# Two-block transformer kernel: weight slots spaced 16 bytes further, operands of two stages shifted, strided weights in one down projection, reversed tokens in another

## The chip, the cores and the metric

The kernel runs on 1 core of one Trainium2 chip. The metric is the device time of one execution in microseconds (us), as a median over runs. TensorE (PE in the rows) does the matmuls; PEld is its weight load. DVE is VectorE, ACT is ScalarE, POOL is GpSimd, SP is SyncE, which issues the weight DMAs.

## What is computed

Two blocks over x of 512 tokens by 1024 features, all float32. Each holds two layers. What matters here is that every matrix product has a large weight matrix, and that the changed stages are the merged output projection and the down projections:

```python
for i in range(2):                                   # first block
    ...
    x = x + rms_norm(merged @ w_out[i], norm_mix_post[i])
    ff = (silu(h @ w_ffn_gate[i]) * (h @ w_ffn_up[i])) @ w_ffn_down[i]    # 2816 -> 1024
    x = x + rms_norm(ff, norm_ffn_post[i])
    e = (p[i] @ w_ple_proj[i]) * sigmoid(x @ w_ple_gate[i])
...
for layer in range(2):                               # second block
    h = h + (hybrid_attention_mixer if layer == 0 else recurrent_mixer)(...)
    u = causal_depthwise_conv(rms_norm(h) @ w_up, conv_w, conv_b)
    g, val = split(u)
    h = h + (gelu(g) * val) @ w_down                  # 3072 -> 1024
```

## The kernel before

Activations lie in SBUF feature-major: a tile `[128, 512]` holds 128 features of all 512 tokens. The weights come as a list of 502 units (`unit_list`), each `[128, 1024]` float32 (4096 bytes per partition): up to 8 blocks of 128 contraction rows by 128 output features. The host lays them out in one array (the helper near L2545).

A unit goes through four slots (`SLOTS = 4`). SP issues the DMA of a unit into `WRAW[:, slot, :]` when the unit four places earlier has been used (L607, semaphore `unit_used`). ACT rounds it to `WHI` in the type fp32r (L1228, `split_of`), POOL computes the remainder `WLO = WRAW - WHI` into the same bytes as `WRAW` (L2383), both three units ahead of their use. Operands are kept as a rounded half and a remainder too: `HH/HL` for the normed input, `MGH/MGL` for the merged branches, `F1H/F1L` and `F2H/F2L` for the hidden layers of the two kinds of feed-forward, `OBH/OBL` (258 columns, so rows 1032 bytes apart) for the Fourier branch, and so on. A product is three matmuls for each block, the helper `three`:

```python
pe.matmul(out_, WHI[w_at], x_hi, start=first, stop=False)      # L621
pe.matmul(out_, WHI[w_at], x_lo, start=False, stop=False)      # L622
return pe.matmul(out_, WLO[w_at], x_hi, start=False, stop=last)  # L623
```

The first argument after the output is stationary (it is loaded by LDWEIGHTS, 128 columns), the second is streamed (512 tokens). In the rows, names behind `<-` stand as streamed operand, stationary operand. `tile(st, j, k, ...)` runs the blocks of one unit into a PSUM bank and marks the unit used. It is called by `out_y`, which runs the stage kinds `out_y` and `residual`: eight output tiles, for F2 three units each (24 blocks). Other stages call `part` or `tile_part`.

The F2 stage stands twice in the program: after the first convolutional feed-forward (from 2443.3 to 2573.8 us of the span, 8 x 24 x 3 = 576 matmuls), whose `residual` has a gain for the next norm, and after the second (3005.3 to 3135.8 us, again 576), whose `residual` has none. F1 stands twice (528 matmuls each), MG twice (192 each).

Work tiles are placed by hand: `place` for the fixed ones (X, HH, HL, WRAW/WLO, WHI, ...), `work(name, shape, at)` at a number of KB behind a base. All start at multiples of 128 bytes before, and a slot is 4096 bytes. `GT` holds a gate in two branch stages: VectorE writes it, ACT applies tanh (L1326, L1373), VectorE reads it (L1877, L1937).

Other places that the prediction speaks of: L697 and L703 (Fourier transform over tokens; L703's stationary operand is `PG[:, s, :, P]`, four columns 1024 bytes apart), L879 (attention scores in plain float32), L913 (probabilities times values, 64 stationary columns), L1055 to L1057 and L1072 to L1074 (the attention input projection, 256 streamed columns), L1115 (sums: 128 stationary columns, one streamed), L1892 and L1894 (the unfolding of the Fourier branch; L1892 writes `MG[:, n, 0:257]` forward, L1894 writes `MG[:, n, 511:256:-1]` backward), L2214 (a tap of the convolution, which reads `U`, rows 2064 bytes apart, at offsets of 4 bytes).

Of the kernel before, what the change touches and what calls it, by code (L numbers as in the profile page):

```python
# [67 lines left out]
BANKS = 4  # L68
LAG = 3
LINE = 128  # L70

F32 = mybir.dt.float32
F32R = mybir.dt.float32r
# [98 lines left out]
class Stage:  # L172
# [3 lines left out]
    def __init__(self, kind, reps, units, tiles, per, *, u0, t0, base, rb=None, width=0, where=None, src=None, dst=None,  # L176
                 gain=None, n=0, stat=False, y=None, gy=None, t=0, made=None, kt=0, first=False, last=False, op=0, mode=None,
                 heads=0, comps=1, out=None, l=0, proj=None, rope=None, qk=None, att=None, norm=None, taps=0, ahead=None, put_off=False):
        self.kind, self.reps, self.units, self.tiles, self.per = kind, reps, units, tiles, per
        self.u0, self.t0, self.base = u0, t0, base  # L180
        self.rb, self.width, self.where = rb, width, where
        self.src, self.dst, self.gain, self.n, self.stat = src, dst, gain, n, stat
        self.y, self.gy, self.t, self.made, self.kt = y, gy, t, made, kt
        self.first, self.last, self.op, self.mode, self.heads, self.comps = first, last, op, mode, heads, comps
        self.out, self.l, self.proj, self.rope, self.qk, self.att = out, l, proj, rope, qk, att
        self.norm, self.taps, self.ahead, self.put_off = norm, taps, ahead, put_off
        self.tables, self.halves, self.begun, self.cq = None, False, False, None

    def at(self, signal, k, r=0):

# [183 lines left out]
def build(nc, wall, wnyq, xin, pin, posi, posc, cols, consts, gmask, dft, dftc, dil, lamv, out_):  # L374


    with ExitStack() as ctx:
# [20 lines left out]
        YH = place("YH", [P, DT, SEQ], at=h_at + 16 * KB)  # L398
        HQ = place("HQ", [P, 16, SEQ], at=h_at)
        w_at = base[0]  # L400
        WRAW = place("WRAW", [P, SLOTS, BLOCKS * P])
        WLO = place("WLO", [P, SLOTS, BLOCKS * P], F32R, at=w_at)
        WHI = place("WHI", [P, SLOTS, BLOCKS * P], F32R)
        SG = place("SG", [P, 4, SEQ])
        SQ, TM = place("SQ", [P, 2, SEQ]), place("TM", [P, 2, SEQ])
        ACC = place("ACC", [P, SEQ])
# [26 lines left out]
        def work(name, shape, at, dt=F32):  # L433
            return place(name, shape, dt, at=s_at + int(at * KB))
# [11 lines left out]
        VCT, VR, KRAW = work("VCT", [P, SEQ], 98), work("VR", [P, ST, P], 26), work("KRAW", [P, SEQ], 8)  # L446
        RBQ, RBK = work("RBQ", [P, SEQ], 76), work("RBK", [P, SEQ], 78)
        PT, PTG, BT = work("PT", [P, 4, SEQ], 28), work("PTG", [P, 4, SEQ], 40), work("BT", [P, 2, ST, 3 * P], 28)
        OCR, OCR2, OAR, GT = work("OCR", [P, 2, SEQ], 22), work("OCR2", [P, 1, SEQ], 48), work("OAR", [P, 4, SEQ], 36), work("GT", [P, SEQ], 100)
        CQH, CQL = work("CQH", [P, 4, SEQ], 28, F32R), work("CQL", [P, 4, SEQ], 36, F32R)  # L450
        QA, KA, VA = work("QA", [P, MLA_H, SEQ], 10), work("KA", [P, MLA_H, SEQ], 44), work("VA", [P, ST, SEQ], 0)
        OCH, OCL = work("OCH", [P, 4, SEQ], 60, F32R), work("OCL", [P, 4, SEQ], 68, F32R)
        OAH, OAL = work("OAH", [P, 4, SEQ], 60, F32R), work("OAL", [P, 4, SEQ], 68, F32R)
        MGH, MGL = work("MGH", [P, DT, SEQ], 28, F32R), work("MGL", [P, DT, SEQ], 44, F32R)
        F1H, F1L = work("F1H", [P, FT1, SEQ], 0, F32R), work("F1L", [P, FT1, SEQ], 44, F32R)
        POH, POL, PROWS = work("POH", [P, 2, SEQ], 92, F32R), work("POL", [P, 2, SEQ], 96, F32R), work("PROWS", [P, ST, PLE], 88)
        YP = work("YP", [P, DT, SEQ], 16)
        QKV, PT2 = work("QKV", [P, ST, 3 * DM], 0), work("PT2", [P, TURNED, SEQ], 48)
        BT2, SGY = work("BT2", [P, 4, SEQ], 72), work("SGY", [P, 2, SEQ], 96)
# [155 lines left out]
        def _(pe):  # L615
# [9 lines left out]
            def tile(st, j, k, r, src, kt, k0=0, ready=None, start=True, stop=True):  # L625

                weights(st.unit(j, r))
                s = st.unit(j) % SLOTS
                if start:
                    pe.wait_ge(bank_free[st.bank(k)], st.use(k, r))  # L630
                hi, lo = src
                for i in range(kt):
                    if ready is not None:
                        pe.wait_ge(S["operand_ready"], ready + k0 + i + 1)
                    mm = three(ps[st.bank(k)][:, :], (slice(None), s, slice(i * P, i * P + P)), hi[:, k0 + i, :],
                               lo[:, k0 + i, :], start and i == 0, stop and i == kt - 1)
                mm.then_inc(unit_used, 1)

            def norm(st):
# [568 lines left out]
        def _(act):  # L1208
# [103 lines left out]
            def fourier_branch(st):  # L1312
                att = st.att
                for q in range(att.heads * ST + DEPTH + 1):
                    n, odd = divmod(q, 2)
                    if q < att.heads * ST:
                        exponentials(att, q)
                    if DEPTH <= q < att.heads * ST + DEPTH:
                        turned_copies(att, q - DEPTH)
                    if q < 2 * DT:  # L1320
                        split_of(st, q)
                    if q <= QT:
                        cq_square(st.cq, q)
                    if n < DT and not odd:
                        act.wait_ge(bank_free[st.bank(3 * n)], st.use(3 * n) + 1)
                        act.activation(GT[:, :], GT[:, :], ACT.Tanh, scale=0.5).then_inc(S["gate_ready"], 1)  # L1326
                    elif n < DT:
                        k = 3 * n + 2
                        act.wait_ge(unit_used, st.unit(2 * n + 1) + 1)
                        if n >= 2:  # L1330
                            act.wait_ge(bank_free[st.bank(k - 7)], st.use(k - 7) + 1)
                        act.activation(TM[:, n % 2, 0:UH], ps[st.bank(k)][:, 0:UH], ACT.Copy, scale=0.5).then_inc(bank_free[st.bank(k)], 1)
# [26 lines left out]
            def branch_mla(st):  # L1359
                att = st.att  # L1360
                for q in range(att.heads * ST + DEPTH + 1):
# [8 lines left out]
                        split_of(st, 2 * r)  # L1370
                    if part_ == 1:
                        act.wait_ge(bank_free[st.bank(2 * r)], st.use(2 * r) + 1)
                        act.activation(GT[:, :], GT[:, :], ACT.Tanh, scale=0.5).then_inc(S["gate_ready"], 1)  # L1373
                    if part_ == 2:
                        split_of(st, 2 * r + 1)
                heads_hi(att, unit_used, st.unit(st.units - 1) + 1)
# [361 lines left out]
        def _(dve):  # L1738
# [123 lines left out]
            def fourier_branch(st):  # L1862
# [3 lines left out]
                for q in range(att.heads * ST + DEPTH + 1):  # L1866
# [6 lines left out]
                    if 1 <= n <= DT and not odd:  # L1873
                        dve.wait_ge(S["gate_ready"], st.at("gate_ready", n))
                        dve.wait_ge(S["unfolded"], st.at("unfolded", n))
                        dve.wait_ge(bank_free[st.bank(3 * n - 2)], st.use(3 * n - 2) + 1)
                        dve.scalar_tensor_tensor(MG[:, n - 1, :], GT[:, :], 1.0, MG[:, n - 1, :], ALU.add, ALU.mult).then_inc(S["product_ready"], 1)  # L1877
                    if q == 2 * DT:
                        dve.wait_ge(S["cq_summed"], st.cq.at("cq_summed", 1))
                        for k, width in ((0, Q_LORA), (1, KV_LORA)):  # L1880
# [2 lines left out]
                    if n < DT and not odd:  # L1883
                        fold_of(st, 2 * n)
                        dve.wait_ge(unit_used, st.unit(2 * n) + 1)
                        if n:
                            dve.wait_ge(S["product_ready"], st.at("product_ready", n))
                        scaled(st, 3 * n, 0, GT[:, :])
                    elif n < DT:
                        even, odd_ = 3 * n + 1, 3 * n + 2  # L1890
                        dve.wait_ge(bank_free[st.bank(odd_)], st.use(odd_) + 1)
# [23 lines left out]
            def branch_mla(st):  # L1915
                att = st.att
                dve.wait_ge(S["factor_rows_ready"], st.at("factor_rows_ready", 0))
                for q in range(att.heads * ST + DEPTH + 1):
# [9 lines left out]
                        dve.scalar_tensor_tensor(MG[:, t, :], TM[:, 0, :], 0.5, MG[:, t, :], ALU.mult, ALU.add).then_inc(S["product_ready"], 1)  # L1928
                    if r < DT - 2 and part_ == 1:
                        dve.wait_ge(unit_used, st.unit(2 * r) + 1)  # L1930
                        scaled(st, 2 * r, 0, GT[:, :])
                    if r < DT - 2 and part_ == 2:
                        dve.wait_ge(unit_used, st.unit(2 * r + 1) + 1)
                        dve.wait_ge(S["gate_ready"], st.at("gate_ready", r + 1))
                        if r:
                            dve.wait_ge(S["product_ready"], st.at("product_ready", r))
                        dve.scalar_tensor_tensor(TM[:, 0, :], GT[:, :], 1.0, ps[st.bank(2 * r + 1)][:, :], ALU.add, ALU.mult)\  # L1937
                           .then_inc(bank_free[st.bank(2 * r + 1)], 1)
                heads_lo(att, st.u0 + st.units - 1, ST)

# [589 lines left out]
def packed_weights(inputs):  # L2530

    w = np.zeros((NU, P, BLOCKS * P), np.float32)
    for n, (name, layer, r0, rows, c0, cols) in enumerate(UNITS):
# [11 lines left out]
            w[n, :, :rows // P * cols] = a.reshape(rows // P, P, cols).transpose(1, 0, 2).reshape(P, -1)  # L2545
        else:
            a = a[r0:r0 + rows, c0:c0 + cols]
            w[n, :, :rows // P * cols] = a.reshape(rows // P, P, cols).transpose(1, 0, 2).reshape(P, -1)
    return w


# [66 lines left out]
```

## Time and profile before

| what | us |
|---|---|
| median of 2 runs | 3156.12 (3155.55 to 3156.69) |
| the profiled execution | 3148.41 |
| its span, first to last instruction | 3146.6 |
| PE busy in the span | 3020.4 (96%) |
| POOL busy | 1476.7 (47%) |
| mean granted clock of TensorE | 0.982 of full |

Busy time of PE counts each matmul to its modelled end, which overlaps the next one; the pace of matmuls is read from their starts, or from the chain of waits, where each piece counts from one start to the next.

### The profile page before, as it was taken

Reading aid. Unit: us, or ns where it says so; the run is one execution under the profiler, and the core shown is the slowest. Engines: PE = TensorE matmul, PEld = TensorE weight load, DVE = VectorE, ACT = ScalarE, POOL = GpSimd, SP = SyncE. Lnnn points to the kernel's source line nnn. Section 1 sums busy time; section 2 is a strip of 40 time slices with the busy share of each in tenths; the row PEclk is TensorE's granted clock in tenths of the full one; section 3 lists DMA queues with packets and bytes.
Section 4 is the critical chain, followed back from the end, with each engine's and each line's share of the span. In section 5 each row is a group of like instructions: output and inputs, shape, how many; then the busy total and the mean of one; then the engine's idle time right before and its main releaser. Section 6 shows DMA issues by size and latency. Waiting matters only on the chain.

```text
span 3146.6 us, 41609 instructions
## 1 busy us (share of the span) xinstructions
PE 3020.4 (96%) x15016; PEld 2465.3 (78%) x15016; DVE 1188.1 (38%) x1996; ACT 1296.4 (41%) x2023; POOL 1476.7 (47%) x851
## 2 busy tenths in 40 slices
PE   8999998999989999999999989889999999999999
PEld 6886786888868776777888779767888877788887
DVE  5444334221062444434221250443555127555510
ACT  3454443232242555443222342563555227344421
POOL 3565455444454654555444444443444434344443
PEclk9999999999989999999999999999999999999999
DMA  3222232333322231332333222102333332233232
GB/s 128 68 81 74 70 121 83 95 96 98 107 74 88 68 93 56 94 101 87 100 93 103 84 86 90 58 1 74 94 100 93 100 94 74 81 100 99 94 98 89
DMA packets 78523, 274.38 MB, mean 87 GB/s; under 512 B 8504, under 2 KB 12216, under 8 KB 78400
## 3 DMA queue, kind: packets, MB, share of 16 engines
q1 hardware_dynamic: 74064, 266.05, 27.5%
q10 hardware_dynamic: 4336, 6.63, 0.6%
q8 instruction: 86, 1.41, 0.2%
q14 instruction: 37, 0.30, 0.0%
HBM read 270.54 MB, written 2.10 MB: 87 GB/s over the span
## 4 chain that ended last, share of the span: by engine, by line
PE 88%; DVE 6%; ACT 3%; issue 1%; POOL 1%; DMA 1%; ACTq 0%; DVEq 0%; SPq 0%
PE ps L621 25%; PE ps L623 24%; PE ps L622 24%; PE ps L879 3%; PE ps L890 2%; PE ps L913 2%; DVE HL L1806 1%; PE ps L1055 1%; PE ps L1057 1%; PE ps L1056 1%; POOL WLO L2383 1%; PE ps L697 1%; DVE ps L1795 1%; DVE X L1798 1%; ACT WHI L1228 1%
## 5 line engine op out<-in xcount | busy, mean ns | idle before, releaser
L2383 POOL TENSOR_TENSOR WLO<-WRAW,WHI 128x1024 fp32r<-128x1024 f32 x471 | 1138.3, 2421 | 1315.7 <-ACT WHI L1228 1315.4
L621 PE MATMUL ps<-HH,WHI 128*128 128x512 f32 x2288 | 909.3, 397 | 46.3 <-DVE HL L1806 23.9
L623 PE MATMUL ps<-HH,WLO 128*128 128x512 f32 x2288 | 896.9, 392 | 0.0
L622 PE MATMUL ps<-HL,WHI 128*128 128x512 f32 x2288 | 896.5, 392 | 0.0
L1228 ACT ACTIVATE WHI<-WRAW 128x1024 fp32r<-128x1024 f32 x471 | 494.8, 1053 | 330.9 <-DMA WRAW<-wall 330.7
L621 PEld LDWEIGHTS ps<-HH,WHI 128*128 128x128 f32 x2288 | 433.0, 189 | 154.7 <-POOL WLO L2383 25.2
L623 PEld LDWEIGHTS ps<-HH,WLO 128*128 128x128 f32 x2288 | 432.9, 189 | 91.3
L622 PEld LDWEIGHTS ps<-HL,WHI 128*128 128x128 f32 x2288 | 433.5, 189 | 88.0 <-issue 1.0
L2214 DVE SCALAR_TENSOR_TENSOR ps<-U,COLS,ps 128x512 f32<-128x512 f32 x192 | 145.1, 755 | 143.8 <-ACT ps L1603 129.7
L1829 DVE TENSOR_TENSOR ACC<-ACC,SQ 128x512 f32<-128x512 f32 x80 | 78.2, 978 | 307.4 <-ACT SQ L1472 293.4
L621 PE MATMUL ps<-F2H,WHI 128*128 128x512 f32 x384 | 149.4, 389 | 0.0
L622 PE MATMUL ps<-F2L,WHI 128*128 128x512 f32 x384 | 149.4, 389 | 0.0
L623 PE MATMUL ps<-F2H,WLO 128*128 128x512 f32 x384 | 149.4, 389 | 0.0
L621 PE MATMUL ps<-F1H,WHI 128*128 128x512 f32 x352 | 137.1, 390 | 0.0
L623 PE MATMUL ps<-F1H,WLO 128*128 128x512 f32 x352 | 137.0, 389 | 0.0
L622 PE MATMUL ps<-F1L,WHI 128*128 128x512 f32 x352 | 136.9, 389 | 0.0
L2465 POOL TENSOR_SCALAR SG<-SG,RS 128x512 f32<-128x512 f32 (+3 forms) x132 | 84.5, 651 | 94.5 <-DVE RS L2066 78.6
L2106 DVE TENSOR_TENSOR X<-X,ps 128x512 f32 x32 | 22.0, 687 | 248.3 <-PE ps L623 248.2
L1055 PE MATMUL ps<-WHI,HH 128*128 128x256 f32 x352 | 101.9, 289 | 6.3 <-POOL WLO L2383 6.3
L1500 ACT ACTIVATE F1H<-TM 128x512 f32 (+1 forms) x44 | 27.8, 631 | 192.8 <-DVE TM L2125 192.8
L1946 DVE TENSOR_TENSOR TM<-ps,RBX 128x512 f32<-128x512 f32 x44 | 30.4, 691 | 189.8 <-PE ps L623 189.8
L1056 PE MATMUL ps<-WLO,HH 128*128 128x256 f32 x352 | 101.3, 288 | 0.0
(367 smaller groups left out, 4684.1 us busy)
## 6 DMA issues: line engine op xcount, KB each, us to landing
WRAW<-wall SPq DMA_DIRECT2D x502, 512.0 KB, 3.6
DFT<-dft ACTq DMA_DIRECT2D x4, 516.0 KB, 5.5
XROWS<-xin SPq DMA_DIRECT2D x2, 1024.0 KB, 7.2
y<-YROWS ACTq DMA_DIRECT2D x4, 512.0 KB, 2.6
PROWS<-pin ACTq DMA_DIRECT2D x2, 512.0 KB, 4.0
DIL<-dil ACTq DMA_DIRECT2D x1, 768.0 KB, 4.9
COLS<-cols ACTq DMA_DIRECT2D x1, 294.5 KB, 6.5
POSI<-posi SPq DMA_DIRECT2D x1, 256.0 KB, 11.7
```

The source lines that it names most:

```text
L621: pe.matmul(out_, WHI[w_at], x_hi, start=first, stop=False)
L622: pe.matmul(out_, WHI[w_at], x_lo, start=False, stop=False)
L623: return pe.matmul(out_, WLO[w_at], x_hi, start=False, stop=last)
L879: pe.matmul(score_bank(st, q, c)[:, 0:(b - a) * P], qs, ks, start=True, stop=True).then_inc(S["scores_ready"], 1)
L890: mm = pe.transpose(turn_ps[c][:, k * P:(k + 1) * P], probs_at(st, q, c)[:, k * P:(k + 1) * P], IDENT[:, :])
L1055: pe.matmul(o, HH[:, t, at], whi, start=t == 0, stop=False)
L1056: pe.matmul(o, HH[:, t, at], wlo, start=False, stop=False)
L1228: act.activation(WHI[:, s, :], WRAW[:, s, :], ACT.Copy).then_inc(wt_hi, 1)
L1829: dve.tensor_tensor(ACC[:, :], ACC[:, :], SQ[:, slot, :], ALU.add).then_inc(S["square_added"], 1)
L2214: dve.scalar_tensor_tensor(d, U[:, k, n - 1 - m:n - 1 - m + SEQ], w(n - 1 - m), src, ALU.mult, ALU.add)\
L2383: pool.tensor_tensor(WLO[:, s, :], whole, WHI[:, s, :].bitcast(F32), ALU.subtract).then_inc(wt_lo, 1)
L2465: pool.tensor_scalar(p, p, RS[:, s:s + 1], 1.0, ALU.mult, ALU.mult).then_inc(S["probs_ready"], 1)
```

## The change

Four edits of addresses and access patterns. No instruction is added, removed or moved: the sequence of instructions and waits on each engine is the same, apart from the name of one tile.

1. Each slot of WRAW, WLO and WHI is followed by 16 unused bytes, so slots are 4112 bytes apart and begin at 0, 16, 32 and 48 bytes behind a multiple of 128 (the sum over four slots is padded to the next multiple of 128).
2. MGH and MGL move 64 bytes down; F1H and F1L move 32 bytes up. F1L then ends where other tiles began, so POH, POL and PROWS move by 512 bytes, and GT is split into GTC and GTA at other places.
3. The weights of the first F2 stage (`ffn_w_down_2`, layer 0) are laid out by the host with the eight blocks interleaved, and the stationary operand takes every eighth element (128 elements, 32 bytes apart).
4. In the second F2 stage the streamed operand and the PSUM output run backward over the 512 tokens; weights are contiguous there.

```diff
+STAGGER = 16
...
+        self.interleaved, self.backwards = src == "F2" and gain is not None, src == "F2" and gain is None
...
-        WRAW = place("WRAW", [P, SLOTS, BLOCKS * P])
-        WLO = place("WLO", [P, SLOTS, BLOCKS * P], F32R, at=w_at)
-        WHI = place("WHI", [P, SLOTS, BLOCKS * P], F32R)
+        unit = slice(0, BLOCKS * P)
+        slots = [P, SLOTS, BLOCKS * P + STAGGER // 4]
+        WRAW = place("WRAW", slots)[:, :, unit]
+        WLO = place("WLO", slots, F32R, at=w_at)[:, :, unit]
+        base[0] += -base[0] % LINE
+        WHI = place("WHI", slots, F32R)[:, :, unit]
+        base[0] += -base[0] % LINE
...
-        OCR, OCR2, OAR, GT = work("OCR", [P, 2, SEQ], 22), work("OCR2", [P, 1, SEQ], 48), work("OAR", [P, 4, SEQ], 36), work("GT", [P, SEQ], 100)
+        OCR, OCR2, OAR = work("OCR", [P, 2, SEQ], 22), work("OCR2", [P, 1, SEQ], 48), work("OAR", [P, 4, SEQ], 36)
+        GTC, GTA = work("GTC", [P, SEQ], 50), work("GTA", [P, SEQ], 82)
...
-        MGH, MGL = work("MGH", [P, DT, SEQ], 28, F32R), work("MGL", [P, DT, SEQ], 44, F32R)
-        F1H, F1L = work("F1H", [P, FT1, SEQ], 0, F32R), work("F1L", [P, FT1, SEQ], 44, F32R)
-        POH, POL, PROWS = work("POH", [P, 2, SEQ], 92, F32R), work("POL", [P, 2, SEQ], 96, F32R), work("PROWS", [P, ST, PLE], 88)
+        MGH, MGL = work("MGH", [P, DT, SEQ], 28 - 1 / 16, F32R), work("MGL", [P, DT, SEQ], 44 - 1 / 16, F32R)
+        F1H, F1L = work("F1H", [P, FT1, SEQ], 1 / 32, F32R), work("F1L", [P, FT1, SEQ], 44 + 1 / 32, F32R)
+        POH, POL, PROWS = work("POH", [P, 2, SEQ], 92.5, F32R), work("POL", [P, 2, SEQ], 96.5, F32R), work("PROWS", [P, ST, PLE], 88.5)
...
-                    mm = three(ps[st.bank(k)][:, :], (slice(None), s, slice(i * P, i * P + P)), hi[:, k0 + i, :],
-                               lo[:, k0 + i, :], start and i == 0, stop and i == kt - 1)
+                    at = slice(i, None, BLOCKS) if st.interleaved else slice(i * P, i * P + P)
+                    tokens = slice(None, None, -1) if st.backwards else slice(None)
+                    mm = three(ps[st.bank(k)][:, tokens], (slice(None), s, at), hi[:, k0 + i, tokens],
+                               lo[:, k0 + i, tokens], start and i == 0, stop and i == kt - 1)
...
-            w[n, :, :rows // P * cols] = a.reshape(rows // P, P, cols).transpose(1, 0, 2).reshape(P, -1)
+            order = (1, 2, 0) if name == "ffn_w_down_2" and layer == 0 else (1, 0, 2)
+            w[n, :, :rows // P * cols] = a.reshape(rows // P, P, cols).transpose(*order).reshape(P, -1)
```

## Rows read from the trace of the kernel before

**Rows 1.** The page, section 1: busy us, share of the span, instructions.

```profile
span 3146.6 us, 41609 instructions
PE 3020.4 (96%) x15016; PEld 2465.3 (78%) x15016; DVE 1188.1 (38%) x1996; ACT 1296.4 (41%) x2023; POOL 1476.7 (47%) x851
```

**Rows 2.** The page, section 4: the chain that ended last.

```profile
PE 88%; DVE 6%; ACT 3%; issue 1%; POOL 1%; DMA 1%; ACTq 0%; DVEq 0%; SPq 0%
```

**Rows 3.** The chain of waits inside the first F2 stage.

```profile
by line: PE ps L622 33.4%; PE ps L621 33.4%; PE ps L623 33.3%
```

**Rows 4.** Stretches MG, F1, F2, F2: us, busy of PE, PEld, DVE, ACT, POOL, PEclk.

```profile
442.00:486.00 44.00, 44.00 (x195) 36.24 (x193) 8.39 (x11) 16.08 (x24) 21.53 (x9) 1.00 0.32 102
744.50:864.00 119.50, 119.50 (x530) 98.93 (x529) 8.10 (x12) 33.67 (x41) 57.42 (x24) 1.00 0.35 106
2443.30:2573.80 130.50, 130.50 (x577) 108.09 (x576) 18.37 (x27) 35.10 (x41) 59.53 (x25) 1.00 0.32 97
3005.30:3135.80 130.50, 130.50 (x577) 107.94 (x575) 8.40 (x12) 24.67 (x25) 54.98 (x23) 1.00 0.28 85
```

**Rows 5.** The chain in order of time, by start: 256 streamed columns in fp32r.

```profile
1872.42 0.12 PE ps L1072
...
1874.82 0.12 PE ps L1074
```

**Rows 6.** Groups by line and form: busy us, mean ns; counts of three-matmul products.

```profile
L621 PE MATMUL ps<-HH,WHI 128*128 128x512 f32 x2288 | 909.3, 397 | 46.3 <-DVE HL L1806 23.9 <-POOL WLO L2383 15.0 <-DVE HL L1809 6.8
L621 PE MATMUL ps<-F2H,WHI 128*128 128x512 f32 x384 | 149.4, 389 | 0.0
L621 PE MATMUL ps<-F1H,WHI 128*128 128x512 f32 x352 | 137.1, 390 | 0.0
L621 PE MATMUL ps<-MGH,WHI 128*128 128x512 f32 x128 | 49.8, 389 | 0.0
```

**Rows 7.** PE in order of time, OBH and OBL: rows 1032 bytes apart.

```profile
136.82 0.28 PE L623 MATMUL ps<-OBH,WLO 128*128 128x258 f32 x1
...
137.89 0.28 PE L623 MATMUL ps<-OBH,WLO 128*128 128x258 f32 x1
```

**Rows 8.** Weight loads by form: minimum/median/maximum ns, or busy us and mean ns.

```profile
L621 PEld LDWEIGHTS ps<-F2H,WHI 128*128 128x128 f32 x384 | 72.1, 188 | 15.1
L913 PEld LDWEIGHTS ps<-PT,VA x512: 132/137/137, 283.5 to 1295.1; 128*64 128x64 f32 x171
L703 PEld LDWEIGHTS ps<-DFT,PG x16: 85/86/90, 113.3 to 1033.0; 128*4 128x4 f32 x16
```

**Rows 9.** The chain in order of time: weight-load-bound sums, plain float32 scores.

```profile
2128.56 3.62 PE ps L1115 x32
288.33 1.72 PE ps L879 x4
```

**Rows 10.** VectorE groups: forward and backward writes, aligned and shifted reads.

```profile
L1892 DVE SCALAR_TENSOR_TENSOR MG<-ps,TM 128x257 f32<-128x257 f32 x16 | 6.8, 428 | 62.2 <-ACT TM L1332 62.2
L1894 DVE SCALAR_TENSOR_TENSOR MG<-ps,TM 128x255 f32<-128x255 f32 x16 | 6.6, 413 | 0.0
L2214 DVE SCALAR_TENSOR_TENSOR ps<-U,COLS,ps 128x512 f32<-128x512 f32 x192 | 145.1, 755 | 143.8 <-ACT ps L1603 129.7 <-DVE ps L2214 3.7
L1795 DVE SCALAR_TENSOR_TENSOR ps<-YH,COLS,ps 128x512 f32<-128x512 f32 x32 | 23.9, 748 | 8.3 <-PE ps L656 8.3
```

**Rows 11.** DMA issues: KB each, median us from issue to landing.

```profile
WRAW<-wall SPq DMA_DIRECT2D x502, 512.0 KB, 3.6
DFT<-dft ACTq DMA_DIRECT2D x4, 516.0 KB, 5.5
```

**Rows 12.** The chain in order of time: a weight DMA on it.

```profile
1986.12 3.66 DMA WRAW<-wall
```

**Rows 13.** Groups: preparing a unit on ACT and POOL.

```profile
L1228 ACT ACTIVATE WHI<-WRAW 128x1024 fp32r<-128x1024 f32 x471 | 494.8, 1053 | 330.9 <-DMA WRAW<-wall 330.7
L2383 POOL TENSOR_TENSOR WLO<-WRAW,WHI 128x1024 fp32r<-128x1024 f32 x471 | 1138.3, 2421 | 1315.7 <-ACT WHI L1228 1315.4
```

More of the change, by code:

```diff
@@ L1325, in fourier_branch @@
                         act.wait_ge(bank_free[st.bank(3 * n)], st.use(3 * n) + 1)
-                        act.activation(GT[:, :], GT[:, :], ACT.Tanh, scale=0.5).then_inc(S["gate_ready"], 1)
+                        act.activation(GTC[:, :], GTC[:, :], ACT.Tanh, scale=0.5).then_inc(S["gate_ready"], 1)
                     elif n < DT:
@@ L1372, in branch_mla @@
                         act.wait_ge(bank_free[st.bank(2 * r)], st.use(2 * r) + 1)
-                        act.activation(GT[:, :], GT[:, :], ACT.Tanh, scale=0.5).then_inc(S["gate_ready"], 1)
+                        act.activation(GTA[:, :], GTA[:, :], ACT.Tanh, scale=0.5).then_inc(S["gate_ready"], 1)
                     if part_ == 2:
@@ L1876, in fourier_branch @@
                         dve.wait_ge(bank_free[st.bank(3 * n - 2)], st.use(3 * n - 2) + 1)
-                        dve.scalar_tensor_tensor(MG[:, n - 1, :], GT[:, :], 1.0, MG[:, n - 1, :], ALU.add, ALU.mult).then_inc(S["product_ready"], 1)
+                        dve.scalar_tensor_tensor(MG[:, n - 1, :], GTC[:, :], 1.0, MG[:, n - 1, :], ALU.add, ALU.mult).then_inc(S["product_ready"], 1)
                     if q == 2 * DT:
@@ L1887, in fourier_branch @@
                             dve.wait_ge(S["product_ready"], st.at("product_ready", n))
-                        scaled(st, 3 * n, 0, GT[:, :])
+                        scaled(st, 3 * n, 0, GTC[:, :])
                     elif n < DT:
@@ L1930, in branch_mla @@
                         dve.wait_ge(unit_used, st.unit(2 * r) + 1)
-                        scaled(st, 2 * r, 0, GT[:, :])
+                        scaled(st, 2 * r, 0, GTA[:, :])
                     if r < DT - 2 and part_ == 2:
@@ L1936, in branch_mla @@
                             dve.wait_ge(S["product_ready"], st.at("product_ready", r))
-                        dve.scalar_tensor_tensor(TM[:, 0, :], GT[:, :], 1.0, ps[st.bank(2 * r + 1)][:, :], ALU.add, ALU.mult)\
+                        dve.scalar_tensor_tensor(TM[:, 0, :], GTA[:, :], 1.0, ps[st.bank(2 * r + 1)][:, :], ALU.add, ALU.mult)\
                            .then_inc(bank_free[st.bank(2 * r + 1)], 1)
```

## The prediction

> **What bounds the kernel now.** I read the page's busy times and its chain first, then the chain inside the changed stages, then those stages' busy times, and last the pace of single matmuls. TensorE is busy for 96% of the span [rows 1] and makes 88% of the chain that ended last, with the DMAs at 1% and POOL at 1% [rows 2]. Inside the first F2 stage the chain is the three matmul lines and nothing else [rows 3]. In the MG, F1 and F2 stages PE is busy for the whole stretch at full granted clock, while POOL, the busiest of the others, has 59.53 of 130.50 us in the first F2 stage [rows 4]. So only what changes the time from one matmul's start to the next can move this kernel by much.
>
> That pace comes from the stretches: 130.50 us for 576 matmuls is 226.6 ns for 512 columns [rows 4]. With 256 columns 20 intervals take 2.40 us, 120.0 ns each [rows 5]. The difference is 106.6 ns for 256 columns, 0.416 ns per column (2.4 GHz, a column per cycle), and what is left is a fixed 13.4 ns per matmul. It is the same at both widths, so it looks like a cost of changing weights, not like a stream that loses cycles all along to the other reader of the memory. There are about 10,560 matmuls of 512 columns in this form: the first of each three for HH, F2, F1 and MG are 2288 + 384 + 352 + 128 [rows 6], times three 9,456, and the smaller products have some 1,100 more. One ns on each is 10.6 us, 0.33% of the time. All of the 13.4 ns is 141 us.
>
> **The change part by part.** No instruction, DMA or wait is added or moved, on SP's and POOL's queues either, so every term is a changed duration.
>
> *Slots 16 bytes apart, MG and F1 shifted.* The nearest rows are those of OBH and OBL, whose rows are 1032 bytes apart, so the streamed operand starts 8 bytes further in each block. Nine intervals take 1.07 us, 118.9 ns each [rows 7], against 120.0 ns for 256 columns that start on a multiple of 128 [rows 5]. Two more columns would cost 0.8 ns, so these are 1.9 ns under what the aligned ones give, within the spread of a stage that is mixed with attention. The ends: 0, and -1.9 ns on all 10,560, or -20 us. From above I know no row in which a start costs anything. One more cycle of 0.4 ns on each would be +4 us, and I keep +10. I take 0: a start at another multiple of 16 bytes is one first access, in front of 512 columns.
>
> *What the slots' other users pay.* ACT's rounding takes 1053 ns, POOL's remainder 2421 ns [rows 13], once per unit of 24 x 226.6 ns = 5.4 us. VectorE reads U at offsets of 4 bytes in 755 ns, aligned YH in 748 ns [rows 10]: under 1% for a shifted start. Even 20% on POOL (0.5 us) stays behind 5.4 us, and shows only where POOL stands on the chain, 1% or 31 us of it [rows 2]: +6 us at most. The DMAs land on 16-byte starts. A weight DMA takes 3.6 us; the DFT table of about the same size takes 5.5 us, in rows of 1032 bytes [rows 11]. Three units ahead, 1.9 us more is hidden behind 16 us of matmuls. On the chain I see four weight DMAs after the start (one in [rows 12]): 4 x 1.9 = +8 us as the upper end. I take 0, since the rows stay 4096 bytes long and only their starts shift.
>
> *GT split.* Same shapes, same waits, other addresses: 0, below and above.
>
> *Interleaved weights in the first F2 stage.* 576 weight loads read 128 elements 32 bytes apart. What a load may cost: where 128 stationary columns serve a single streamed one, 32 of them take 3.62 us, 113 ns each [rows 9]. That is the pace of loads alone. Beside 226.6 ns of matmul it may double to 226 ns before anything is late; the load is the cover's whole question. What the stride costs: a load lasts 188 ns for 128 columns and 137 for 64, 0.80 per column, which gives 89 ns for four contiguous ones; the four columns of L703, 1024 bytes apart, take 86 ns, 90 at most [rows 8]. So 0 to 0.3 ns per column more, at most 38 ns on a load: 151 ns, still hidden. Ends: 0 below. From above, the slowest rate at which an engine here takes float32 elements is POOL's 2421 / 1024 = 2.36 ns [rows 13]: a load of 303 ns, (303 - 226.6) x 576 = +44 us. L703's four columns might be absorbed at the load's start, so I go beyond that, to an assumed load four times as long: 4 x 113 = 452 ns per matmul, (452 - 226.6) x 576 = +130 us. I take 0, by the row that has a stride.
>
> *Backward tokens in the second F2 stage.* 576 matmuls stream 512 columns and write PSUM in descending order. No row shows TensorE do this. On VectorE L1894 writes backward, 255 elements in 413 ns (1.62 each); L1892 writes forward, 257 in 428 ns (1.67 each) [rows 10]. From above the nearest row is a matmul at half rate, the plain float32 scores: 1.72 us for four, 430 ns each [rows 9]. Half rate would be (430 - 226.6) x 576 = +117 us. Below nothing I see no reason. Neighbours in descending order touch the same bytes as neighbours in ascending order, and VectorE shows no cost, so I take 0, with less trust than in the other parts. The stage ends the program: the last tile is stored after it, so nothing covers a loss.
>
> **A rule weighed.** The stride first: L703 shows none [rows 8]. The Trainium skill, Advanced Engine Details and Errata, SBUF Cachelines, says that accesses need at least two hits on a 16-byte line to absorb the memory's latency, and that another line per access costs. By that, the interleaved load, with one hit per line, is slower by an amount it doesn't give; at twice 113 ns it would still hide, and at the quadruple it is the +130 us above. By this row, no cost.
>
> **The sum.** 0 + 0 + 0 + 0 + 0 on the profiled execution of 3148.4 us (3146.6 of span and 1.8 around it). The median of the runs is 3156.1, 7.7 us higher; the forecast is given on that scale: 3156. Edges of this case: -20 for all starts at the pace of [rows 7], giving 3136; +10, +6 and +8 for starts, POOL and DMAs, giving 3180.
>
> **The rivals.**
>
> *Backward is slow (slower).* The mechanism is one: TensorE's stream or its PSUM writes handle two neighbours at once only in ascending order, and a descending step falls to one per two cycles. Place: the 576 matmuls from 3005.3 us. Price: 117 us, so 3156 + 117 = 3273, +3.7%. It decides from 63 us on (2%), that is from a pace of 336 ns. For it: a column per 0.416 ns is the fastest stream in this kernel, and plain float32 runs at half of it, so there is a slower regime to fall into; for VectorE, at 1.6 ns per element, order may not matter where it does for TensorE. Against: the backward pair touches the same bytes as the forward one. The Trainium skill says in the same page, PSUM Cachelines, that any non-contiguous pattern significantly slows matmuls and that every two consecutive elements should be contiguous; whether descending neighbours count is not said, and no row of this trace shows it.
>
> *Interleaved loads are slow (slower).* A strided column costs four times a contiguous one: 3156 + 130 = 3286. At three times, 339 ns, it would be (339 - 226.6) x 576 = 65 us, 3221, just over 2%; so it needs a factor of three. For it: only that L703 has few columns. Against: L703's 86 ns and the half of the weight port's time that is free. With the first rival together: 3403.
>
> *Slots in phase were the 13.4 ns (faster).* If the fixed cost is a collision between a weight load and the stream, both on multiples of 128 bytes, three of four slots would lose it: 0.75 x 141 = 106 us, giving 3050, -3.4%. For it: the plain float32 matmul takes 430 ns [rows 9], only 3.6 over twice the 213.2 of its stream, and it loads weights as well, so a lower fixed cost exists. Against: OBH's starts at 8-byte steps keep nearly all of it (118.9 - 107.3 = 11.6 ns) [rows 7].
>
> **How the numbers follow.** No measurable difference, 3136 to 3180: 0.60. Backward slow, about 3273: 0.26. Interleave slow, 3221 to 3286, alone or with the other: 0.07. Faster by the slots: 0.05. Others small on either side: 0.02. Predicted time 3156, of the likeliest. The range must take in the backward case to leave no more than 2 in 10 out: 3136 to 3280 (the likeliest alone: 3136 to 3180). By over 2%, 63 us, about what a measurement of this kernel can tell from no change: faster 0.06, within 0.61, slower 0.33.
>
> **What would show it.** After, the pace in the F2 stages: 130.5 us each if both patterns are free; 247 us in the last one if backward runs at half rate (a PE busy stretch that long, the chain still all matmuls); in the first one over 195 us, with PEld durations far above 188 ns and above the pace, if the stride costs. PEld at 200 to 300 ns with a pace of 227 would mean that it costs and is hidden. In the H stages 226.6 ns or 225; at 216 the slot rival is right. A weight DMA over 4 us or POOL's remainder over 2.5 us would show that the starts matter there. The forecast is wrong if any 576 matmuls take over 190 us, or if the pace of H falls under 222 ns.

## The result, and the profile after

The changed kernel takes 3212.59 us (median of 2 runs, 3210.55 to 3214.62), the kernel before 3156.12. The ratio is 1.0179, 95% interval 1.0135 to 1.0223: slower by 56.5 us, clear of noise, while the interval leaves open whether it is more or less than 2%. The forecast was 3156, with all terms at 0; 3212.59 lies inside the range of 3136 to 3280, but neither of the two slow rivals as priced is what happened.

After is read in the order in which before was. First the page: span and busy times (section 1), the chain (section 4).

```profile
span 3212.8 us, 41609 instructions
PE 3080.9 (96%) x15016; PEld 2495.5 (78%) x15016; DVE 1188.8 (37%) x1996; ACT 1297.1 (40%) x2023; POOL 1474.1 (46%) x851
...
PE 88%; DVE 6%; ACT 2%; issue 1%; POOL 1%; DMA 1%; ACTq 0%; DVEq 0%; SPq 0%
```

Against [rows 1, 2] the instruction counts are the same, PE is busy for 60.5 us more, its weight loads for 30.2 us more, and the others for no longer than before; the chain has nearly the same shares. It isn't waits that were added in the main: single matmuls became slower. The chain of waits inside the first F2 stage, against [rows 3]:

```profile
by line: PE ps L630 33.6%; PE ps L629 33.3%; PE ps L628 33.2%
```

The same stretches as [rows 4] in the changed kernel, and between MG and F1 the swiglu feed-forward stage on HH and HL (972 of its matmuls). Columns: stretch, its length, busy of PE, PEld, DVE, ACT, POOL, granted clock, DMA share, GB/s.

```profile
446.70:491.20 44.50, 44.50 (x193) 35.85 (x191) 8.33 (x11) 15.81 (x23) 21.41 (x9) 1.00 0.30 98
526.90:754.80 227.90, 226.74 (x976) 182.57 (x975) 60.09 (x85) 67.89 (x86) 99.61 (x42) 1.00 0.30 94
755.60:878.60 123.00, 123.00 (x531) 99.27 (x530) 8.15 (x13) 33.65 (x41) 57.62 (x24) 1.00 0.33 103
...
2486.50:2627.90 141.40, 141.40 (x578) 141.36 (x578) 18.37 (x27) 34.60 (x40) 59.50 (x25) 1.00 0.28 90
3067.00:3202.00 135.00, 135.00 (x577) 108.02 (x575) 8.41 (x12) 24.48 (x24) 54.39 (x23) 1.00 0.26 82
```

The clock is full in each, so it is no clock effect. In the first F2 stage 141.40 us for 576 matmuls is 245.5 ns each, and PEld is busy for 141.36 of 141.40 us (before 108.09 of 130.50): weight loads now have no gap. In the second it is 135.00 / 576 = 234.4 ns, with PEld as idle as before. F1 and MG, neither interleaved nor backward, went from 226.7 to 232.9 ns (123.00 / 528) and 231.8 ns (44.50 / 192).

Here is the same stretch of the swiglu stage in the kernel before:

```profile
521.50:743.60 222.10, 220.75 (x976) 182.41 (x975) 60.07 (x85) 67.90 (x86) 99.27 (x42) 1.00 0.32 97
```

No edit names this stage's operand; its 972 matmuls take 5.8 us more, 6 ns each. Added up from start to start over the profiled executions, the products on HH and HL with 512 streamed columns (6864 matmuls) account for +34.2 us, the two F2 for +15.3, F1 for +6.5 and MG for +2.2: 58 of the 66.2 us between the two spans. Another +4.2 us lies in 64 matmuls of 128 columns in the attention (L1099, before L1090). It isn't of this kind: TensorE sits idle there for VectorE longer than before (20.2 us, before 8.2), and the granted clock of the stretch is 0.79, before 0.88. The weight load groups in the two F2 stages of after, as in [rows 8]:

```profile
L628 PEld LDWEIGHTS ps<-F2H,WHI 128*128 128x128 f32 x192 | 63.4, 330 | 0.0
...
L629 PEld LDWEIGHTS ps<-F2L,WHI 128*128 128x128 f32 x192 | 36.1, 188 | 9.1
```

The interleaved load lasts 330 ns, in the backward stage it is 188 as before. The users of the slots, as in [rows 11, 13]:

```profile
WRAW<-wall SPq DMA_DIRECT2D x502, 512.0 KB, 3.5
...
L2392 POOL TENSOR_TENSOR WLO<-WRAW,WHI 128x1024 fp32r<-128x1024 f32 x471 | 1135.8, 2416 | 1376.1 <-ACT WHI L1237 1375.7
L1237 ACT ACTIVATE WHI<-WRAW 128x1024 fp32r<-128x1024 f32 x471 | 494.5, 1052 | 338.3 <-DMA WRAW<-wall 338.0
```

They pay nothing. What is open, then: 6 ns on every 512-column product. The slots are the only edit that touches all of them.

### The profile page after: what moved, and what is told of

Same layout as the page of the kernel before. It is cut to its first block, busy times and chain, and to the rows that moved or that the text cites. A ratio compares the mean times of both kernels' runs of the same rounds, so it can differ in the third digit from the quotient of the medians.

```text
span 3212.8 us, 41609 instructions
## 1 busy us (share of the span) xinstructions
PE 3080.9 (96%) x15016; PEld 2495.5 (78%) x15016; DVE 1188.8 (37%) x1996; ACT 1297.1 (40%) x2023; POOL 1474.1 (46%) x851
## 4 chain that ended last, share of the span: by engine, by line
PE 88%; DVE 6%; ACT 2%; issue 1%; POOL 1%; DMA 1%; ACTq 0%; DVEq 0%; SPq 0%
PE ps L628 25%; PE ps L629 24%; PE ps L630 24%; PE ps L888 3%; PE ps L899 2%; PE ps L922 2%; DVE HL L1815 1%; PE ps L1064 1%; PE ps L1065 1%; PE ps L1066 1%; PE ps L706 1%; POOL WLO L2392 1%; DVE ps L1804 1%; DVE X L1807 1%; PE ps L917 0%
## 5 line engine op out<-in xcount | busy, mean ns | idle before, releaser
L2392 POOL TENSOR_TENSOR WLO<-WRAW,WHI 128x1024 fp32r<-128x1024 f32 x471 | 1135.8, 2416 | 1376.1 <-ACT WHI L1237 1375.7
L628 PE MATMUL ps<-HH,WHI 128*128 128x512 f32 x2288 | 919.8, 402 | 47.6 <-DVE HL L1815 25.2
L629 PE MATMUL ps<-HL,WHI 128*128 128x512 f32 x2288 | 907.6, 397 | 0.0
L1237 ACT ACTIVATE WHI<-WRAW 128x1024 fp32r<-128x1024 f32 x471 | 494.5, 1052 | 338.3 <-DMA WRAW<-wall 338.0
L630 PEld LDWEIGHTS ps<-F2H,WLO 128*128 128x128 f32 x384 | 99.5, 259 | 9.1
L628 PEld LDWEIGHTS ps<-F2H,WHI 128*128 128x128 f32 x384 | 99.5, 259 | 8.7
```

What stands on the lines that cost most here:

```text
L1237: act.activation(WHI[:, s, :], WRAW[:, s, :], ACT.Copy).then_inc(wt_hi, 1)
L2392: pool.tensor_tensor(WLO[:, s, :], whole, WHI[:, s, :].bitcast(F32), ALU.subtract).then_inc(wt_lo, 1)
```

## The experiments

"Pace" is the mean time from one matmul's start to the next in a stage, of 512-column products; 226.7 ns is what all stages have before.

### Each edit alone

`e1_slots_only` holds edit 1 and the split of GT, `e2_shift_only` edit 2 (with the split), `e3_patterns_only` edits 3 and 4; the lines are those of the diff above. The split of GT is also in e4 to e8 and e11 to e14.

> Edit 1 alone (slots 16 bytes further apart, GT split because the work tiles move up), all else as before. Theory A (the start of the weights against a multiple of 128 bytes costs time on each matmul): the pace of the H, F1, MG and both F2 stages rises from 226.6 ns to about 232.5, the sum is +60 us or so, near 3216. Theory B (the loss sits in the shifted operands and the two patterns, the slots only carry it): under +10 us, near 3160.

> Edit 2 alone (MG 64 bytes down, F1 32 bytes up, slots as before). Theory A in the form that only the distance between weights and stream counts: the MG stages (384 matmuls) and F1 stages (1056) go to about 232 ns, +8 us in all. Theory A in the form that only the weights' start counts, or theory B' (shifts cost nothing at all): 226.6 ns stays everywhere, 3156.

> Edits 3 and 4 alone, slots and operands as before. In the changed kernel the interleaved stage ran at 245.5 ns and the backward one at 234.5, where its H stages ran at 232.6. If the patterns have a cost of their own: about 240 ns in the first F2 stage (+13 on 576, +7.5 us) and about 228.5 in the second (+1 us), near 3165. If the patterns cost only together with unequal starts: 226.6 in both, 3156.

| run | us (runs) | ratio, 95% | pace H / MG / F1 / F2 / F2 |
|---|---|---|---|
| slots only | 3205.51 (4) | 1.0163 (1.0146 to 1.018) | 232.8 in all |
| shift only | 3165.47 (7) | 1.0032 (1.002 to 1.0043) | 226.7 / 233.3 / 233.3 / 226.7 / 226.7 |
| patterns only | 3167.76 (6) | 1.0044 (1.003 to 1.0059) | 226.7 / 226.7 / 226.7 / 244.7 / 233.3 |
| all (the change) | 3212.59 (2) | 1.0179 (1.0135 to 1.0223) | 232.8 / 232 / 232.9 / 245.5 / 234.4 |

The first F2 stage with the slots alone; F1 and the first F2 stage with the shift alone; both F2 stages with the patterns alone:

```profile
2484.10:2618.30 134.20, 134.20 (x578) 108.20 (x577) 18.36 (x27) 34.59 (x40) 59.76 (x25) 1.00 0.30 94
```

```profile
747.00:870.20 123.20, 123.20 (x530) 99.01 (x529) 8.15 (x13) 33.64 (x41) 57.56 (x24) 1.00 0.34 103
...
2463.20:2593.70 130.50, 130.50 (x577) 108.09 (x576) 18.34 (x27) 35.05 (x41) 59.53 (x25) 1.00 0.31 97
```

```profile
2444.40:2585.30 140.90, 140.90 (x577) 140.90 (x577) 18.35 (x27) 35.07 (x41) 59.48 (x25) 1.00 0.29 90
...
3016.60:3151.00 134.40, 134.40 (x577) 108.11 (x576) 8.40 (x12) 24.67 (x25) 54.39 (x23) 1.00 0.26 82
```

The slots alone make nearly the whole loss (51 us over the 3154.43 of its comparison), in every stage. The shift costs just the two stages whose operands it moves, the patterns just theirs. The three losses, by their ratios 51 + 10 + 14 = 75 us, are more than the 56 of all together: MG, F1 and the backward stage, off by 6 ns through the slots, do not pay those 6 ns a second time.

### What in the slots costs: the spacing, or where WHI came to lie

The spacing also moves what lies behind. WRAW and WLO begin at byte 49280 of a partition, which is 128 past a multiple of 256; so did WHI (65664) and every streamed operand of these products before. Four slots of 4112 bytes are 16448, padded to 16512, an odd multiple of 128: WHI begins at 65792, a multiple of 256. It moved by 128 bytes against WLO and the operands (what lies behind it moved by 256, so it kept its place modulo 256). Three kernels take this apart: slots 128 bytes apart (`STAGGER = 128`, where WHI stays in place), slots 16 apart with WHI kept, and WHI moved alone.

```diff
 e5, WHI kept (on top of the slots-only kernel; twice)
-        base[0] += -base[0] % LINE
+        base[0] += (w_at - base[0]) % 256
```

```diff
 e6, WHI moved alone (on top of the kernel before)
+        base[0] += 128
         WHI = place("WHI", [P, SLOTS, BLOCKS * P], F32R)
+        base[0] += 128
```

> As edit 1, but the slots are 128 bytes further apart instead of 16: every start stays on a multiple of 128, while slots and all later tiles move. Theory A (the phase within 128 bytes counts): 226.6 ns everywhere, 3156. Rival C (the distance between slots or the new places of the tiles count, not the phase): over 230 ns, 3200 or more.

> As edit 1, but WHI keeps its start 128 above a multiple of 256 bytes as before; in the change the padding to 128 moved WHI by 128 against WRAW, WLO and the operands. Theory P (the distance between the loaded weights and the streamed operand within 256 bytes counts, 0 is the cheap one): slot 0 (distance 0) at 226.7 ns, slots 1 to 3 (16, 32, 48 bytes) at 233 ns, so about 231.5 in the H stages. Rival R (only the 128-byte move of WHI made the loss, 16 bytes cost nothing): 226.7 in all slots.

> Slots 4096 bytes apart as before, WHI alone 128 bytes further up. Theory P: two of the three matmuls of each block load from WHI while H streams, at distance 128, so 230 to 233 ns everywhere. Rival S (only differences among the slots count, a common move of WHI doesn't): 226.7.

Measured: e4 3182.98 us (ratio 1.009, 1.0073 to 1.0107), pace 230.2 over all, which is 227 in slots 0 and 2 and 232.8 in slots 1 and 3. e5 3182.11 against 3154.66, again 230.2. e6 3212.32 against 3154.66, 233.3 everywhere. None of the expected pictures fits e4: the multiple of 128 isn't what counts, and a slot 256 bytes on is fast again. In e5 theory P holds but for slot 1, which stays fast at 16 bytes. PE in order of time in e5, first F2 stage; each pair of rows is 24 matmuls apart, a unit, the first pair in slot 3 and the second in slot 1:

```profile
2484.07 0.40 PE L627 MATMUL ps<-F2H,WHI 128*128 128x512 f32 x1
...
2489.68 0.40 PE L627 MATMUL ps<-F2H,WHI 128*128 128x512 f32 x1
...
2494.91 0.39 PE L629 MATMUL ps<-F2H,WLO 128*128 128x512 f32 x1
...
2500.35 0.40 PE L629 MATMUL ps<-F2H,WLO 128*128 128x512 f32 x1
```

5.61 / 24 = 233.8 ns in one unit, 5.44 / 24 = 226.7 in another: the pace changes from slot to slot. Slots at 0 and 16 bytes run at 226.7, those at 32 and 48 at 233.3. And the first F2 stage of e6, with slots 4096 apart:

```profile
2490.30:2624.70 134.40, 134.40 (x577) 108.18 (x576) 18.38 (x27) 34.57 (x40) 59.47 (x25) 1.00 0.30 94
```

So 128 bytes between WHI and the rest cost 57.7 us, as much as the whole change; the spacing as such costs 27.5 (one run each). What moves the pace is the distance between where the weights and where the stream begin. It doesn't act product by product: a third of the products in e6 load WLO, which stayed in place, and they are as slow as the others (232 to 235 ns to the next start, whichever of the three lines). Were only the two thirds with WHI slow, the mean would be 231.1 ns, and it is 233.3.

The same lines put in the changed kernel give its loss without the accident of WHI's place.

> The changed kernel with one thing undone: WHI starts at 128 above a multiple of 256 again, as WRAW, WLO and the operands do. By the paces so far: H 230.2 instead of 232.8 (-2.6 ns on about 7,900 matmuls, -20 us), MG and F1 232 to 233 as now, the interleaved stage about 245 and the backward one about 234 as now: 3190 against 3212. If the 16-byte spacing alone were to blame the time would stay at 3210.

It takes 3193.37 us against 3155.66 (ratio 1.0119, 1.0102 to 1.0136): 37.7 us slower than before where the change is 56.5, so WHI's place is worth about 19 us inside the change. Its swiglu stage, F1 and the first F2 stage:

```profile
526.80:752.20 225.40, 224.11 (x974) 182.91 (x973) 60.04 (x85) 67.94 (x86) 99.20 (x42) 1.00 0.30 95
753.00:873.70 120.70, 120.70 (x531) 99.16 (x529) 8.19 (x13) 33.65 (x41) 57.47 (x24) 1.00 0.33 105
...
2470.00:2611.30 141.30, 141.30 (x577) 141.28 (x577) 18.36 (x27) 34.73 (x41) 59.44 (x25) 1.00 0.28 90
```

The time is as expected, but F1 is not: 120.70 / 528 is 228.6 ns, where 232 to 233 was expected. F1 lies 32 bytes up and the slots at 0, 16, 32 and 48, so its stream is at +32, +16, 0 and -16 against the weights. PE in order of time in F1, each pair a unit of 24 matmuls, the first in slot 0 (+32), the second in slot 2 (0):

```profile
773.66 0.39 PE L628 MATMUL ps<-F1H,WHI 128*128 128x512 f32 x1
...
779.25 0.39 PE L628 MATMUL ps<-F1H,WHI 128*128 128x512 f32 x1
...
783.33 0.39 PE L628 MATMUL ps<-F1H,WHI 128*128 128x512 f32 x1
...
788.77 0.39 PE L628 MATMUL ps<-F1H,WHI 128*128 128x512 f32 x1
```

5.59 / 24 = 232.9 ns, against 5.44 / 24 = 226.7. In slot 2 stream and weights both begin 32 bytes off a multiple of 128, and the pace is the fast one: it is the distance that counts, not each start by itself.

### A map of distances

Slots as before, operands moved by different amounts per stage. For e7:

```diff
+        base[0] += 128        # ahead of the normed input: H +128
-        MGH, MGL = work("MGH", [P, DT, SEQ], 28, F32R), ...
+        MGH, MGL = work("MGH", [P, DT, SEQ], 28 - 128 / KB, F32R), ...
-        F1H, F1L = work("F1H", [P, FT1, SEQ], 0, F32R), ...
+        F1H, F1L = work("F1H", [P, FT1, SEQ], 64 / KB, F32R), ...
-        F2H, F2L = work("F2H", [P, FT2, SEQ], 0, F32R), ...
+        F2H, F2L = work("F2H", [P, FT2, SEQ], 32 / KB, F32R), ...
```

e8 has H +32, MG -192, F1 +128, F2 +96; e11 H +64, MG -32, F1 +192, F2 +64, and the second F2 stage backward. e12 has all slots 16 bytes up (still 4096 apart), MG -64, F1 +32, F2 +96; e13 has all slots 16 bytes up and no operand moved.

> Slots as before; operands moved by stage: H up by 128 bytes, MG down by 128, F1 up by 64, F2 up by 32. Theory P with 256 bytes: all four stages leave 226.7, to about 233. Rival Q (what counts is a start off a multiple of 128, wherever): H and MG stay at 226.7, F1 and F2 go to 233. Rival T (a stream whose start is moved never costs, only weights' starts do) is out already by the run with shifts alone (233.3 ns in MG and F1).

> Slots as before; H up by 32 bytes, MG down by 192, F1 up by 128, F2 up by 96. Theory P: all at 233 or so, MG too. A distance that is better than 0 would show here as a pace under 226.7. Rival Q: F1 stays at 226.7, the others at 233.

> Slots as before; H and F2 up by 64 bytes, F1 up by 192, MG down by 32, and the second F2 stage backward. If the pace goes by the distance between weights and stream alone, whatever tile it is: H and the first F2 stage about 229 ns as F1 was at 64, F1 233.3 as MG was at -64, MG 233.3. For the backward stage: theory D (backward costs only because its first read lies at another distance): another value than 233.3, down to 227 to 229. Theory E (descending order costs by itself, +6.6): 233.3 again or more, up to 236.

> All slots 16 bytes up, 4096 apart; MG down by 64, F1 up by 32, F2 up by 96 bytes. The stream then starts 16 bytes below the weights for H (modulo 256), 80 below for MG, 16 above for F1, 80 above for F2. If 16 bytes either way are free (slot 1 of the run with WHI kept was at 226.7): H and F1 226.7. MG and F2 between 229 and 233.3. A stage under 226.7 would give a layout that beats the kernel before.

> All slots 16 bytes up and 4096 apart, every operand where it was: one distance (16 bytes) in all stages. Theory P (the distance decides): 226.7 ns in every long stage, as in slot 1 of the run with WHI kept, 3156. Rival G (the distance allows two steady paces, and what precedes a stage decides which it falls into): some long stages at 226.9 and others, the second convolutional H stage first, at 233.3, between 3165 and 3195.

Times, one run each: e7 3196.33 and e8 3200.59 against 3154.66; e11 3174.69 and e12 3174.49 against 3154.41; e13 3176.43 against 3155.66. The paces, with those of e2, e5, e6 and e14:

| stream minus weights, modulo 256 | pace, ns | seen in |
|---|---|---|
| 0 | 226.7 | before, all stages |
| +16 | 226.7 | e12 F1; e14 F1, slot 1 |
| -16 | 226.7 | e5, slot 1; e14 F1, slot 3 |
| -16 | 226.7 or 233.3, by stage | e12 H; e13 |
| +32, -32, -48 | 233.3 | e2, e7, e8, e11, e5 |
| +64 | 228.9 to 229.0 | e7 F1, e8 MG, e11 H and F2 |
| -64 | 233.3 | e2 MG, e11 F1 |
| -64 to -112, by slot | 233.0 | e14 MG |
| +80 / -80 | 230.0 / 232.0 | e12 F2 / MG |
| +96 | 233.3 | e8 F2 |
| 128 | 232.4 | e7 H, e8 F1 (moved up) |
| 128 | 233.3 | e7 MG (moved down); e6 (WHI alone) |

F1 at +64 in e7, and MG at +64 (-192) in e8:

```profile
755.90:876.80 120.90, 120.90 (x531) 99.24 (x529) 8.19 (x13) 33.65 (x41) 57.66 (x24) 1.00 0.33 105
```

```profile
446.50:490.50 44.00, 44.00 (x193) 35.88 (x191) 8.36 (x11) 15.80 (x23) 21.50 (x9) 1.00 0.30 98
```

No distance gives less than 226.7, so nothing here beats the kernel before. Theory P of e7 and e8 (about 233 at any distance but 0) was too coarse: +64 costs a third of that. Rival Q is out, since H and MG lose at 128. In e7, H, MG and F1 lose while WHI and WLO keep their distance from each other, so it is not that distance either. The distance modulo 256 is not all of it. 128 up and 128 down differ by 0.9 ns, and in e13 both F2 stages have one operand tile, one set of slots and one distance, -16:

```profile
2459.30:2589.80 130.50, 130.50 (x577) 108.09 (x576) 18.36 (x27) 35.07 (x41) 59.70 (x25) 1.00 0.31 97
...
3029.40:3163.80 134.40, 134.40 (x577) 108.65 (x576) 8.41 (x12) 24.52 (x24) 55.16 (x23) 1.00 0.26 82
```

The first runs at 226.7 throughout, the second at 233.3 throughout. In e13 the swiglu and first convolution stages and F1 are fast too; MG, the first H stage and the second convolution stage are slow, and the H products of the recurrent part have both. So rival G is what e13 shows, as far as the two paces go. What picks one of the two paces I have not found; it stays open.

e11 also tells whether the backward cost is such a distance effect. Its F2 stages, both at +64, forward and backward:

```profile
2462.20:2594.00 131.80, 131.80 (x577) 108.17 (x576) 18.36 (x27) 34.86 (x41) 59.80 (x25) 1.00 0.31 96
...
3027.70:3162.10 134.40, 134.40 (x577) 108.10 (x575) 8.39 (x12) 24.52 (x25) 54.35 (x23) 1.00 0.26 82
```

Backward takes 233.3 ns here as at distance 0; only the forward stage reacts to the distance. A pace of 233.3 is where backward lies in both, as theory E said. Whether the stream or the PSUM writes make it slow wasn't separated.

With 256 streamed columns the distance acts the other way. The attention input projection (L1055 to L1057) has the normed input stationary and streams 128 columns from each of two slots. Its long stretch before, in the changed kernel and in e12:

```profile
1896.50:1985.50 89.00, 89.00 (x744) 89.00 (x743) 5.12 (x8) 30.36 (x50) 31.59 (x14) 1.00 0.25 83
```

```profile
1926.50:2013.00 86.50, 86.50 (x736) 86.50 (x735) 4.85 (x8) 30.10 (x50) 30.94 (x13) 1.00 0.24 86
```

```profile
1908.50:1995.00 86.50, 86.50 (x744) 86.50 (x743) 5.12 (x8) 30.30 (x50) 31.42 (x14) 1.00 0.25 86
```

From start to start that is 120.0 ns before, 118.0 in the changed kernel and 116.7 in e12; the other runs with moved slots or a moved H lie between 117.8 and 118.7, and e6, e2 and e9 at 120.0. PEld has no gap in these three, so the loads may be what sets this pace; that was not tested. So the distance that is best with 512 columns isn't best here.

### Is the fixed 13.4 ns the weight load?

e9 loads fewer weight columns: 64 in the first F2 stage, 32 in the second. The remaining output features are not computed.

```diff
+        self.columns = (64 if gain is not None else 32) if src == "F2" else P
...
+                    n = st.columns
-                    mm = three(ps[st.bank(k)][:, :], (slice(None), s, slice(i * P, i * P + P)), hi[:, k0 + i, :],
+                    mm = three(ps[st.bank(k)][0:n, :], (slice(None), s, slice(i * P, i * P + n)), hi[:, k0 + i, :],
```

> As before, but the F2 stages load only 64 (first) and 32 (second) of the 128 stationary columns, so 64 and 96 of each 128 output features aren't computed. Theory F (the 13.4 ns over the stream is a fixed cost per matmul): 226.6 ns in both stages. Theory L (the load takes cycles of the stream's memory, in proportion to its columns: 13.4 for 128): 220.0 ns and 216.7 ns, the stages 127 and 125 us instead of 130.5.

```profile
2448.30:2580.80 132.50, 132.50 (x578) 77.35 (x577) 18.35 (x27) 35.05 (x41) 59.83 (x25) 1.00 0.31 96
...
3011.80:3145.20 133.40, 133.40 (x577) 62.59 (x575) 8.40 (x12) 24.62 (x25) 55.17 (x23) 1.00 0.27 83
```

Loads of 134 and 109 ns instead of 188, and the pace did not fall: 230.0 and 231.7 ns, slower than 128 columns and what neither theory F (226.6) nor L (220.0 and 216.7) had; 3157.88 us against 3154.41. If each weight read took a beat from the stream, a half or a quarter of the columns would have shortened it. So the 13.4 ns isn't a sum over loaded columns.

### What a stride of the weights costs

e10 takes every second column of two blocks in the first F2 stage (8 bytes apart) and every fourth of four in the second (16 apart), without laying the weights out for it, so the products use the wrong weights.

```diff
+        self.step = (2 if gain is not None else 4) if src == "F2" else 1
...
+                    n = st.step
+                    at = slice(i // n * n * P + i % n, (i // n + 1) * n * P, n)
```

> As before, but the stationary operand takes every second element (8 bytes apart) in the first F2 stage and every fourth (16 bytes apart) in the second; the weights aren't laid out for it, so these products aren't the reference's. At 32 bytes apart a load lasted 330 ns and the pace was 244.7. Theory W (only one element per 16 bytes is dear, two are not): load 188 ns and pace 226.7 at 8 bytes, 330 and 244.7 at 16 bytes. Rival V (the load slows with the distance, per byte passed): 8 bytes about 208 ns, 16 bytes about 250, paces 226 to 235. Rival X (any stride but 1 is dear): 330 ns and 244.7 in both.

It takes 3165.16 us against 3154.41 (one run). Weight loads of the first, then of the second F2 stage, and the windows:

```profile
L622 PEld LDWEIGHTS ps<-F2H,WHI 128*128 128x128 f32 x174 | 33.6, 193 | 7.0
...
L622 PEld LDWEIGHTS ps<-F2H,WHI 128*128 128x128 f32 x175 | 54.2, 309 | 0.0
```

```profile
2450.80:2585.20 134.40, 134.40 (x577) 111.17 (x577) 18.35 (x27) 35.09 (x41) 59.43 (x25) 1.00 0.30 94
...
3017.10:3152.50 135.40, 135.40 (x577) 135.23 (x576) 8.40 (x12) 24.69 (x25) 55.03 (x23) 1.00 0.26 82
```

In duration of a load: 188 ns at 4 bytes, 193 at 8, 309 at 16, 330 at 32. The step is between 8 and 16. The traces agree with the rule weighed before, of at least two hits on a 16-byte line (the Trainium skill, Advanced Engine Details and Errata, SBUF Cachelines): with two hits a load lasts 5 ns longer, with one 121 ns longer. At 16 bytes PEld is full and the pace is the load's, 235 ns. At 8 bytes it isn't full and the pace is 233.3 all the same; weights there begin at other distances too, and the two weren't separated. Theory W has the durations right to 7%, but not the paces (226.7 and 244.7 expected, 233.3 and 235.0 measured).

## Why the prediction was right or wrong

**Bound: right.** PE's pace bounds the kernel, and nearly the whole difference is in it. Neither of its signs of being wrong occurred ("if any 576 matmuls take over 190 us, or if the pace of H falls under 222 ns"), yet the forecast was wrong: a small rise of the pace over all stages was not among the signs. One ns on all 10,560 had been priced at 10.6 us, and 6 ns is what came.

**The range: luck.** It reaches to 3280 for the backward case, which did not happen. 3212.59 lies in the gap between the likeliest case (to 3180) and the rivals (from 3221), which had 0.02 for both sides together.

**Slots: the step that failed.** "I take 0: a start at another multiple of 16 bytes is one first access, in front of 512 columns", with +10 us as the upper end. Measured: +51 us. Three things failed in it. The edit was read as a spacing of slots, while padding also moved WHI by 128 bytes against WLO and the operands, which alone costs 57.7 us (e6). The start was taken by itself, where the distance between weights and stream counts. And the nearest row was of the wrong width: OBH's 258 columns [rows 7] at 118.9 ns showed no cost, and at that width there is none. The attention projection at 256 columns went from 120.0 to 118.0 ns in the changed kernel, where all 512-column stages lose 6 ns. The -1.9 ns read from OBH has the sign and about the size of that, and it doesn't carry over to 512 columns.

**The 13.4 ns: the reasoning behind it failed as well.** The 13.4 ns is "the same at both widths, so it looks like a cost of changing weights, not like a stream that loses cycles all along to the other reader of the memory." At 512 columns it becomes 20 ns by distance alone (233.3 over the 213.3 of the stream), at 256 it shrinks to 11.4 (118.0 over 106.6). That it was the same at both widths says nothing: it is what two widths leave once the cost per column has been worked out from their difference. e9 speaks against loaded columns as its source; a fixed cost per change of weights would not depend on width. Neither theory holds, and what the 13.4 ns are stays open.

**Rival "slots in phase were the 13.4 ns": right that distance matters, wrong in sign.** With 512 columns in phase is the best case found, not the collision; with 256 its sign is right, by 2 ns.

**Slots' other users, GT: right.** 3.5 us per DMA, 1052 and 2416 ns; shift only, which holds the GT split, loses only in MG and F1.

**Interleaved weights: 0 taken, about +10.4 us measured** (140.90 against 130.50), between the 0 and the +130 given. The term was mis-sized by "L703's 86 ns": four columns say nothing on 128. PEld full at 245.5 ns per load, 1.92 ns a column against 113 / 128 = 0.88 for contiguous ones: a factor of 2.2, just past the factor of two up to which it hides. For the time of a load, the bound from POOL's rate (303 ns) had been nearer than the 151 ns from the row with the stride.

**Backward: 0 taken, +3.9 us measured** (134.40 against 130.50; 6.8 ns each). The rival's half rate, 430 ns, is out. That it would be nothing like the rival's 117 us was right; that it is nothing was wrong by one step of the pace.

**Not additive.** A sum of terms was the wrong form: a second cause adds little to the first where the stage already has the slower pace (backward: 233.3 ns alone, 234.4 with the slots, which alone give 232.8).

## What to carry to other kernels

An edit of addresses is costed by writing out where every tile lands afterwards, those behind the edited one too: here the padding moved a tile nobody named. In this form of matmul with 512 streamed columns keep the stationary and the streamed operand at one position modulo 256 bytes, and weights contiguous: 8 bytes apart already had the pace of 233.3, 16 and 32 bytes are bound by the load. A row bounds an unknown cost only if it has the same width and the same partner: four columns showed none of it, and 256 instead of 512 had the other sign.

## What was unexpected of the hardware

- With 512 streamed fp32r columns the pace depends on the distance between weights and stream modulo 256 bytes: 226.7 ns at 0, 228.9 at +64, 226.7 at +16, 230.0 at +80, 232 to 233.3 at most others. At 2.4 GHz 226.7 ns is 544 cycles and 233.3 is 560. Why was not shown.
- At -16 bytes one stage keeps 226.7 for all its 576 matmuls and another of the same tiles 233.3. The cause is open.
- Weight loads of 64 and 32 columns (134, 109 ns) give a pace of 230.0 and 231.7, not under 226.7.
- A backward stream with backward PSUM writes takes 233.3 ns at distance 0 and at +64 alike.
- With 256 streamed columns distance 0 is the slow case: 120.0 ns, against 116.7 to 118.7 where slots or H were moved. The weights moved by 128 alone (e6) leave it at 120.0.
